# Product-key experts: one-hot tiles with the token innermost and 16-bit operands, weight streams in 1 MB halves

## The chip, the core and the metric

The kernel runs on one core of one Trainium2 chip. Its time is the device time of one launch in microseconds (us); the lower the better. Engines are named as in the profile: PE (TensorE matmuls), PEld (TensorE weight loads), DVE (VectorE), ACT (ScalarE), POOL (GpSimd), SP (the queue that issues the DMAs).

## The reference, cut to what matters

The program is two layers of a mixing stage and a product-key expert stage, then one further mixer and a mixture of 32 experts. The change touches the product-key stage (`_peer`). For 256 tokens, 8 heads and 16 picks a head, it is

```
s    = einsum('thcd,ckd->thck', q, subkeys)        # 2 x 128 key scores a head
sv, si = top_k(s, 16);  cand = sv[..0..] + sv[..1..];  cv, ci = top_k(cand, 16)
experts = ea * 128 + eb                            # ea, eb in 0..127: 16384 experts
gate = softmax(cv)
act  = gelu(einsum('cd,ced->ce', x, u_tab[experts]))
y    = einsum('ce,ced->cd', act * gate, v_tab[experts])
```

Each token uses 128 of the 16,384 experts, and every expert has a row of 1024 numbers in `u_tab` and one in `v_tab`, all float32.

## The kernel before, in words

The product-key stage gathers nothing. It goes through all 16,384 experts in 128 chunks (chunk c holds the experts with second key c, 128 of them, one for each first key), for all 256 tokens, and multiplies by a gate that is zero where a token did not pick an expert. Three kinds of work run on PE:

- **stage 1** (`pe_stage1`, L979): chunk c of `u` times the tokens, float32, 8 products of 128x128 by 128x256, which the profile lists as 16 matmuls. ACT puts the gelu into the slot `c % 76` of the store `H` (`HELD` is 76).
- **build** (`pe_build`, L989): the gates of 16 tokens for 32 chunks. For token i the product of a one-hot over the 128 first keys (`Aoh`) with a one-hot over 32 second keys times the gate (`Boh`, the gate cut into three bf16 parts, k = 0 to 2) gives a 128x32 tile; 16 tokens times 3 parts are 48 matmuls, 128x128 by 128x32 in bf16. There are 64 builds a layer, n = 0 to 63: builds 16q to 16q + 15 are for chunks 32q to 32q + 31. The 128 lanes of `Aoh` and `Boh` are the picks of a token. DVE makes `Aoh` in `dve_keys_hot` (one comparison of 2048 elements a lane) and `Boh` in `dve_gates_hot` (one comparison and three products of 512 elements), and multiplies the built gates into `H` in `dve_gate`. `Aoh`, `Boh` and the result banks are held twice.
- **stage 2** (`pe_stage2`, L998): chunk c of `H` times chunk c of `v`, each cut in a high and a low part by ACT and DVE (`act_split_v`, `dve_split_v`, `dve_split_p`), 12 matmuls of 512 columns. `dve_split_v` of chunk c + 2 waits for stage 2 of chunk c, since `v_lo` is held twice.

The order is written out by hand. PE runs stage 1 for chunks 0 to 31, then 16 times a build and one or two chunks of stage 1 (chunks 32 to 49), and then a loop over c = 0 to 127 of stage 2, into which the other builds and chunks 50 to 127 of stage 1 are put: two chunks of stage 1 for each c up to 24, then one for each c up to 52, and none after that. Builds 16 to 31 stand at c = 8 to 23, builds 32 to 47 at c = 25 to 40, and builds 48 to 63 at every 2.4 chunks from c = 55 to c = 91. DVE makes the first keys' one-hots one or two chunks ahead of the build and the gates' one-hots one chunk ahead. Engines work through their own instruction lists in order, and wait for each other by semaphores.

The weights come through a ring of three places of 2 MB (`Slots`, `load`): a DMA brings four chunks of `u` (when stage 1 comes to a multiple of four) or of `v`, strictly in the order of the list on SP, and each waits until the place's earlier tenant has been given back, which is at the last of its four chunks (`ring.back`). In the loop the order on SP is two pieces of `u` and one of `v` for four chunks. A piece of `v` is given back by `dve_split_v`. While SP waits for one place it issues nothing behind it.

In the arena, `eg` (numbers of the picked keys and gates, float32) and `gs` (the three gate parts, float32) lie in front of `H`; slots of `H` from 50 on (`ROUTED`) lie over the routing scratch, so that gelus from chunk 50 on wait until the routing is over.

Of the kernel before, what the change touches and what calls it, by code (L numbers as in the profile page):

```python
# [17 lines left out]
NSLOT = 3  # L18
PIECE = 4096
HELD = 76  # L20
TURNED = 19
BEFORE = 50
ROUTED = 50
FREE = 1 << 20
# [206 lines left out]


def bc(ap, axis, n):
    ap = ap.unsqueeze(axis)
    shape = list(ap.shape)
    shape[axis] = n
    return ap.broadcast_to(shape)


def build(nc, d, out):  # L240
    with ExitStack() as ctx:
# [50 lines left out]

        ring = Slots([ring_t[:, i * PIECE:(i + 1) * PIECE] for i in range(NSLOT)], at)
        s_ring = [sem(f"ring{i}_landed") for i in range(NSLOT)]
        fills = [0] * NSLOT
        banks = Slots(bank, at)
# [3 lines left out]
        def load(src, cols, *key):  # L300
            buf, (s, n) = ring.take(*key)
            i = ring.place[key]
            fills[i] += 1
            S.wait_ge(s, n)
            S.dma(buf[:, 0:cols], src, s_ring[i])
            at.put(("landed", key), s_ring[i], 16 * fills[i])
# [136 lines left out]
        def pe_mod(j):  # L443
            if j % 6:
                pe_mod_turn(j - 1)
            b, (s, n) = banks.take("mod", j)
            P.wait_ge(s, n)
            P.wait_ge(*at["landed", ("w_mod", j)])
            P.wait_ge(*at["silu c"])
            w = ring.of("w_mod", j).rearrange("p (c n) -> p c n", c=8)  # L450
# [106 lines left out]
        def pe_project_out(l, k, yT, *made):  # L557
            P.wait_ge(*at[made])
            P.wait_ge(*at["landed", ("w_out", l, k)])
            w = ring.of("w_out", l, k).rearrange("p (c n) -> p c n", c=4)  # L560
            for tk in range(2):
                for dh in range(2):
                    b, (s, n) = banks.take("out", l, k, tk, dh)
                    P.wait_ge(s, n)
                    P.mm(b[:, :], [(yT[:, c, tk * 128:tk * 128 + 128], w[:, c, dh * 512:dh * 512 + 512]) for c in range(4)])
                    P.mark("out", l, k, tk, dh)
            ring.back(P, "w_out", l, k)

        def pe_mixing(l):
# [5 lines left out]
            for j in range(4):  # L575
                P.wait_ge(*at["landed", ("w_inA", l, j)])
                w = ring.of("w_inA", l, j).rearrange("p (c n) -> p c n", c=8)
                for half in range(2):
# [338 lines left out]
        top[0] = ARENA - 11200  # L917
        assert H0 + 256 * ROUTED <= top[0]
        pq = [ar3(4, 256) for _ in range(2)]
        ps_ = [ar4(2, 4, 128) for _ in range(4)]  # L920
# [58 lines left out]
        def pe_stage1(l, c):  # L979
            P.wait_ge(*at["landed", ("u", l, c // 4)])  # L980
            if c >= 2:
                P.wait_ge(*at["gelu", l, c - 2])
            w = ring.of("u", l, c // 4).rearrange("p (i c a) -> p i c a", i=4, c=8)
            P.mm(bU[c % 2][:, 0:256], [(w[:, c % 4, dc, :], xT[:, dc, :]) for dc in range(8)])
            P.mark("up", l, c)
            if c % 4 == 3:
                ring.back(P, "u", l, c // 4)
# [22 lines left out]
        def pe_peer(l):  # L1010
            after_stage(P, "mix", l)
            route_banks.restart()
            for j in range(4):
                P.wait_ge(*at["landed", ("wq", l, j)])
                w = ring.of("wq", l, j).rearrange("p (c n) -> p c n", c=8)
                for hf in range(2):
# [120 lines left out]
        def dve_split_v(l, c):  # L1137
            w = ring.of("vt", l, c // 4).rearrange("p (i n) -> p i n", i=4)[:, c % 4, :]
            V.wait_ge(*at["v high", l, c])
# [3 lines left out]
            V.mark("v split", l, c)  # L1143
            if c % 4 == 3:
                ring.back(V, "vt", l, c // 4)

        def dve_peer(l):
# [15 lines left out]
            V.cp(gsb[:, 0, :], eg[:, 2, :])  # L1163
            V.cp(gs[:, 0, :], gsb[:, 0, :])
# [3 lines left out]
            V.tt(gs[:, 2, :], eg[:, 2, :], gs[:, 1, :], SUB)  # L1168
            V.mark("gates split", l)
            for n in range(16):  # L1170
                dve_keys_hot(l, n)
# [48 lines left out]
        def act_split_v(l, c):  # L1220
            A.wait_ge(*at["landed", ("vt", l, c // 4)])
            if c >= 3:
                A.wait_ge(*at["down", l, c - 3])
            A.act(v_hi[c % 3], ring.of("vt", l, c // 4).rearrange("p (i n) -> p i n", i=4)[:, c % 4, :], ACT.Copy)
            A.mark("v high", l, c)
# [41 lines left out]
        def pool_peer(l):  # L1267
            after_stage(G, "mix", l)
            end_stage(G, "G", "peer", l)

# [89 lines left out]
        def pe_task(kind, k, ct):  # L1360
            P.wait_ge(*at["landed", ("w_hg", kind, k)])
            w = ring.of("w_hg", kind, k).rearrange("p (c n) -> p c n", c=8)
            cs = slice(ct * 128, ct * 128 + 128)
# [114 lines left out]
        def pe_mixer():  # L1478
# [16 lines left out]
            P.wait_ge(*at["ckv"])  # L1495
            w = ring.of("w_kvb").rearrange("p (v c n) -> p v c n", v=2, c=2)
            for h in range(8):
# [506 lines left out]
        more_slots = [ar(PIECE) for _ in range((ARENA - top[0]) // PIECE)]  # L2004
        s_ring += [sem(f"ring{NSLOT + i}_landed") for i in range(len(more_slots))]
        top[0] = e_mark
# [28 lines left out]
        def sp_moe():  # L2035
# [4 lines left out]
            once(bgu[0:32, :], d["b_gu"], "b_gu")  # L2040
            for i in range(len(more_slots)):
                ring.bufs.append(more_slots[i])
                ring.tenant.append(None)
                fills.append(0)
            ring.n = NSLOT
            load(d["w_gu"][0, 3], 4096, "w_gu", 0, 1, 1)
# [51 lines left out]
        def pe_up(j, i, k, *gathered):  # L2098
            x = xe[i]
            for v in range(2):  # L2100
# [7 lines left out]
                for h in range(2):  # L2108
                    P.wait_ge(*at["landed", ("w_gu", j, v, h)])
                    w = ring.of("w_gu", j, v, h).rearrange("p (c g n) -> p c g n", c=4, g=2)  # L2110
                    for c in range(4):
# [20 lines left out]
        def pe_down(j):  # L2132
# [3 lines left out]
            for hf in range(2):  # L2136
                P.wait_ge(*at["landed", ("w_dn", j, hf)])
                w = ring.of("w_dn", j, hf).rearrange("p (f n) -> p f n", f=4)
                for f in range(4):
# [375 lines left out]
        def start_ring():  # L2515
            ring.bufs, fills[:] = ring.bufs[0:NSLOT], [0] * NSLOT
            ring.restart()
# [183 lines left out]
```

## Time and profile before

| | before |
|---|---|
| median of 3 runs | 4366.12 us (4361.21 to 4377.41) |
| the profiled execution: time, span | 4377.61 us, 4375.8 us |
| mean granted TensorE clock | 0.944 |
| PE busy | 3942.4 us (90%) |
| DVE busy | 2018.1 us (46%) |
| ACT busy | 895.2 us (20%) |
| POOL busy | 154.4 us (4%) |

The span is one execution, from its first to its last instruction. Busy times are those of instructions that compute; a share is an average over stages with different limits. The product-key stage of the first layer lies at about 250 to 1300 us of the span, that of the second at about 1500 to 2530 us, and the last 1100 us are the 32 experts. The granted clock is 1.00 at the full 2.4 GHz and 0.50 at 1.2 GHz.

### The profile page before, as it was taken

The numbers are of one execution on the slowest core, as the hardware profiler recorded it, in microseconds if no ns is written. First come the engines' busy times: TensorE is split into PE (matmuls) and PEld (weight loads), VectorE is DVE, ScalarE is ACT, GpSimd is POOL, SyncE is SP. The second block draws the span as 40 slices with busy tenths as digits, with TensorE's granted clock in tenths as the row PEclk, the third lists the DMA queues.
The fourth block names the chain that finished last, engine by engine and source line by source line (L and its number), as shares of the span: only waits on it lengthen the run. The fifth ranks groups of instructions, "written<-read, shape, count | busy, mean of one in ns | idle before, by whom it ended". The sixth has DMA issues, their size and how long they took to land.

```text
span 4375.8 us, 54878 instructions
## 1 busy us (share of the span) xinstructions
PE 3942.4 (90%) x23468; PEld 2746.5 (63%) x23468; DVE 2018.1 (46%) x3441; ACT 895.2 (20%) x1502; POOL 154.4 (4%) x135
## 2 busy tenths in 40 slices
PE   6989999998988899999998979998869999999986
PEld 5778878886777688887876756565643333332333
DVE  4276645748754497255758533355532111111112
ACT  2311111223434111212233421223300000000000
POOL 0000000000000000000000000021200000000000
PEclk9799999999998899999999989999979999999998
DMA  4433323443344333333443331211129999999993
GB/s 182 155 135 138 132 116 131 159 155 135 135 165 155 134 137 125 124 136 135 154 154 123 137 127 49 106 58 58 58 81 413 427 428 427 428 427 428 425 398 145
DMA packets 62282, 846.18 MB, mean 193 GB/s; under 512 B 6800, under 2 KB 8976, under 8 KB 10160
## 3 DMA queue, kind: packets, MB, share of 16 engines
q1 hardware_dynamic: 62032, 842.60, 47.9%
q8 instruction: 187, 3.06, 0.3%
q14 instruction: 63, 0.52, 0.0%
HBM read 841.52 MB, written 1.05 MB: 193 GB/s over the span
## 4 chain that ended last, share of the span: by engine, by line
PE 67%; DVE 15%; DMA 13%; ACT 3%; issue 2%; SPq 0%; POOL 0%; DVEq 0%; ACTq 0%
PE bank L83 65%; DVE arena L119 6%; DMA ring<-in_w_gu_dram 6%; DMA ring<-in_peer_u_dram 3%; DMA arena<-in_w_gu_dram 3%; ACT arena L109 2%; DVE vlo L119 2%; PE bank L96 2%; DVE arena L187 1%; DVE arena L181 1%; DVE arena L193 1%; DVE arena L145 1%; DVE arena L133 1%; DVE arena L125 1%; DVE arena L127 1%
## 5 line engine op out<-in xcount | busy, mean ns | idle before, releaser
L83 PE MATMUL bank<-xT,ring 128*128 128x256 f32 x5120 | 1174.1, 389 | 55.7 <-DMA ring<-in_peer_u_dram 33.4
L83 PEld LDWEIGHTS bank<-xT,ring 128*128 128x128 f32 x5120 | 988.2, 195 | 197.8 <-DMA ring<-in_peer_u_dram 35.9
L83 PE MATMUL bank<-arena 128*128 128x32 bf16 (+7 forms) x9660 | 926.6, 291 | 145.7 <-DVE arena L119 108.5
L83 PEld LDWEIGHTS bank<-arena 128*128 128x128 bf16 (+4 forms) x9660 | 544.4, 126 | 522.9 <-issue 294.5
L83 PE MATMUL bank<-ring,arena 128*64 128x512 f32 (+1 forms) x2304 | 592.5, 606 | 39.5 <-DMA ring<-in_w_gu_dram 33.7
L109 ACT ACTIVATE arena<-bank 128x256 f32<-128x256 f32 (+2 forms) x484 | 223.8, 462 | 1975.2 <-PE bank L83 1484.6
L83 PEld LDWEIGHTS bank<-ring,arena 128*64 128x64 f32 (+1 forms) x2304 | 194.4, 146 | 427.3 <-issue 328.5
L119 DVE TENSOR_TENSOR arena<-arena 128x512 bf16<-128x512 bf16 (+6 forms) x636 | 424.4, 703 | 82.0 <-ACT arena L109 67.9
L119 DVE TENSOR_TENSOR vlo<-ring,vhi 128x1024 fp32r<-128x1024 f32 x256 | 313.2, 1224 | 267.2 <-PE bank L83 249.8
L83 PE MATMUL bank<-vhi,phi 128*128 128x512 f32 x1024 | 432.3, 422 | 0.0
L83 PE MATMUL bank<-vhi,plo 128*128 128x512 f32 x1024 | 406.7, 397 | 0.0
L83 PE MATMUL bank<-vlo,phi 128*128 128x512 f32 x1024 | 406.6, 397 | 0.0
L83 PE MATMUL bank<-arena,ring 128*128 128x256 f32 (+2 forms) x1472 | 363.3, 409 | 26.6 <-issue 14.2
L119 DVE TENSOR_TENSOR arena<-cst,arena 128x2048 bf16<-128x2048 f32 (+1 forms) x257 | 372.4, 1481 | 0.0
L83 PEld LDWEIGHTS bank<-arena,ring 128*128 128x128 f32 (+1 forms) x1472 | 253.1, 188 | 129.0 <-issue 91.4
L109 ACT ACTIVATE arena<-arena 128x512 f32<-128x512 f32 (+7 forms) x202 | 134.4, 666 | 797.8 <-DVE arena L125 619.0
L109 ACT ACTIVATE vhi<-ring 128x1024 fp32r<-128x1024 f32 x256 | 272.0, 1063 | 31.4 <-DMA ring<-in_peer_v_dram 20.3
L119 DVE TENSOR_TENSOR plo<-arena,phi 128x256 fp32r<-128x256 f32 x256 | 107.9, 421 | 318.2 <-ACT phi L109 318.2
L139 DVE COPY arena<-bank 128x256 f32<-128x256 f32 (+4 forms) x124 | 70.3, 567 | 387.9 <-PE bank L83 337.1
L83 PEld LDWEIGHTS bank<-vhi,plo 128*128 128x128 f32 x1024 | 197.1, 192 | 44.0
L83 PEld LDWEIGHTS bank<-vlo,phi 128*128 128x128 f32 x1024 | 198.0, 193 | 40.3
L83 PEld LDWEIGHTS bank<-vhi,phi 128*128 128x128 f32 x1024 | 197.5, 193 | 39.6
(105 smaller groups left out, 1665.9 us busy)
## 6 DMA issues: line engine op xcount, KB each, us to landing
ring<-in_w_gu_dram SPq DMA_DIRECT2D x85, 2048.0 KB, 19.3
ring<-in_peer_u_dram SPq DMA_DIRECT2D x64, 2048.0 KB, 8.7
ring<-in_peer_v_dram SPq DMA_DIRECT2D x64, 2048.0 KB, 8.6
arena<-in_w_gu_dram SPq DMA_DIRECT2D x55, 2048.0 KB, 19.4
ring<-in_w_dn_dram SPq DMA_DIRECT2D x41, 2048.0 KB, 17.9
arena<-in_w_dn_dram SPq DMA_DIRECT2D x29, 2048.0 KB, 20.6
ring<-in_w_hg_dram SPq DMA_DIRECT2D x14, 2048.0 KB, 8.6
ring<-in_w_mod_dram SPq DMA_DIRECT2D x12, 2048.0 KB, 7.8
```

The costliest lines, as they stand in the source:

```text
L83: i = self.e.matmul(o, l, r, start=start, stop=stop)
L96: self.e.transpose(o, src, ident[0:n, 0:n]).then_inc(self.sem, 1)
L109: self.e.activation(o, i, f, scale=scale, **kw).then_inc(self.sem, 1)
L119: self.e.tensor_tensor(o, a, b, op).then_inc(self.sem, 1)
L125: self.e.tensor_scalar(o, a, s1, None, o1).then_inc(self.sem, 1)
L127: self.e.tensor_scalar(o, a, s1, s2, o1, o2).then_inc(self.sem, 1)
L133: self.e.scalar_tensor_tensor(out=o, in0=a, scalar=s, in1=b, op0=o1, op1=o2).then_inc(self.sem, 1)
L139: self.e.tensor_copy(o, i).then_inc(self.sem, 1)
L145: self.e.tensor_reduce(o, i, AX.X, op, negate=neg).then_inc(self.sem, 1)
L181: self.e.max(o, i).then_inc(self.sem, 1)
L187: self.e.max_index(o, v, i).then_inc(self.sem, 1)
L193: self.e.match_replace(o, v, i, by).then_inc(self.sem, 1)
```

## The change

- `Aoh`, `Boh` and the comparison tile `eqb` are laid out with the token innermost: an element (key, token) lies at 16 * key + token, where it was at 128 * token + key (32 * token + key for `Boh` and `eqb`). What DVE reads for them becomes bf16 too: `e16` in place of `eg`, `gsb` in place of `gs`, and `keys16`, a bf16 list in which each key's number stands 16 times, in place of `iota`. POOL writes `keys16` once a layer, at the head of the stage; one more DVE copy makes `e16`.
- PE reads one token's one-hots as columns that lie 16 elements (32 bytes) apart, for the stationary operand (128 columns) and for the moving one (32 columns). The number and the order of all matmuls stay.
- The ring has six half places of 1 MB. `u` and `v` come in DMAs of two chunks, 64 and 64 a layer where it was 32 and 32, and each waits for the tenant of its own half. A load of more than 1 MB takes two neighbouring halves, and waits for both.
- `eg` and `gs` move behind `H`, into the scratch; `ROUTED` goes from 50 to 45.

```diff
 PIECE = 4096
+HALF = PIECE // 2
-ROUTED = 50
+ROUTED = 45
...
+class Ring:
+    def __init__(self, places, at):
+        self.places, self.at, self.place = list(places), at, {}
+        self.restart()
+    def restart(self):
+        self.n, self.tenant = 0, [None] * (2 * len(self.places))
+    def take(self, cols, *key):
+        wide = cols > HALF
+        if wide and self.n % 2:
+            self.n += 1
+        i = self.n % len(self.tenant)
+        self.n += 1 + wide
+        before = [k for k in self.tenant[i:i + 1 + wide] if k]
+        self.tenant[i:i + 1 + wide] = [key] * (1 + wide)
+        self.place[key] = i
+        return i, [self.at["back", k] for k in before]
...
         def load(src, cols, *key):
-            buf, (s, n) = ring.take(*key)
-            i = ring.place[key]
+            i, before = ring.take(cols, *key)
             fills[i] += 1
-            S.wait_ge(s, n)
-            S.dma(buf[:, 0:cols], src, s_ring[i])
+            for s, n in before:
+                S.wait_ge(s, n)
+            S.dma(ring.half(i)[:, 0:cols], src, s_ring[i])
...
-        eg = ar4(3, 2, 128).rearrange("p k t n -> p k (t n)")
-        gs = ar4(3, 1, 256).rearrange("p k o n -> p k (o n)")
         gsb = ar(384).bitcast(BF16).rearrange("p (k n) -> p k n", k=3)
+        e16 = ar(256).bitcast(BF16).rearrange("p (c n) -> p c n", c=2)
+        keys16 = ar(1024).bitcast(BF16).rearrange("p (a t) -> p a t", t=16)
...
-        Aoh = [ar(1024).bitcast(BF16).rearrange("p (t a) -> p t a", t=16) for _ in range(2)]
-        Boh = [ar(768).bitcast(BF16).rearrange("p (k t b) -> p k t b", k=3, t=16) for _ in range(2)]
-        eqb = [ar(256).bitcast(BF16).rearrange("p (t b) -> p t b", t=16) for _ in range(2)]
-        top[0] = ARENA - 11200
+        Aoh = [ar(1024).bitcast(BF16).rearrange("p (a t) -> p a t", t=16) for _ in range(2)]
+        Boh = [ar(768).bitcast(BF16).rearrange("p (k b t) -> p k b t", k=3, t=16) for _ in range(2)]
+        eqb = [ar(256).bitcast(BF16).rearrange("p (b t) -> p b t", t=16) for _ in range(2)]
+        top[0] = ARENA - 12736
...
         def sp_u(l, c):
-            if c % 4 == 0:
-                load(d["peer_u"][l, c // 4], 4096, "u", l, c // 4)
+            if c % 2 == 0:
+                load(d["peer_u"][l, c // 4][:, c % 4 * 1024:c % 4 * 1024 + 2048], 2048, "u", l, c // 2)
 
         def sp_v(l, c):
-            if c % 4 == 0 and c < 128:
-                load(d["peer_v"][l, c // 4], 4096, "vt", l, c // 4)
+            if c % 2 == 0 and c < 128:
+                load(d["peer_v"][l, c // 4][:, c % 4 * 1024:c % 4 * 1024 + 2048], 2048, "vt", l, c // 2)
...
-                P.mm(bG[n % 2][:, i * 32:i * 32 + 32], [(ah[:, i, :], bh[:, k, i, :]) for k in range(3)])
+                P.mm(bG[n % 2][:, i * 32:i * 32 + 32], [(ah[:, :, i], bh[:, k, :, i]) for k in range(3)])
...
-            V.tt(Aoh[n % 2], bc(iota, 1, 16), bc(eg[:, 0, t0:t0 + 16], 2, 128), EQ, lag=FREE)
+            V.tt(Aoh[n % 2], keys16, bc(e16[:, 0, t0:t0 + 16], 1, 128), EQ, lag=0 if n < 2 else FREE)
...
-            V.tt(eqb[n % 2], bc(iota[:, q * 32:q * 32 + 32], 1, 16), bc(eg[:, 1, t0:t0 + 16], 2, 32), EQ, lag=FREE)
+            V.tt(eqb[n % 2], keys16[:, 32 * q:32 * q + 32, :], bc(e16[:, 1, t0:t0 + 16], 1, 32), EQ, lag=FREE)
...
-                V.tt(Boh[n % 2][:, k, :, :], eqb[n % 2], bc(gs[:, k, t0:t0 + 16], 2, 32), MUL, lag=k)
+                V.tt(Boh[n % 2][:, k, :, :], eqb[n % 2], bc(gsb[:, k, t0:t0 + 16], 1, 32), MUL, lag=k)
...
         def pool_peer(l):
             after_stage(G, "mix", l)
+            G.cp(keys16, bc(iota, 2, 16))
+            G.mark("keys listed", l)
```

`pe_stage1`, `act_split_v` and `dve_split_v` take their chunk from a half place and give it back at every odd chunk, `dve_peer` waits for "keys listed" ahead of its first comparison, and all other users of the ring read the first 2 MB from their place as before.

## Rows read from the trace of the kernel before

**Rows 1.** The page: busy time of each engine over the whole span.

```profile
PE 3942.4 (90%) x23468; PEld 2746.5 (63%) x23468; DVE 2018.1 (46%) x3441; ACT 895.2 (20%) x1502; POOL 154.4 (4%) x135
```

**Rows 2.** Stretches of the first product-key stage: length, busy us, clock, DMA share, GB/s.

```profile
core 0: us, PE busy (x) PEld busy (x) DVE busy (x) ACT busy (x) POOL busy (x), PEclk, DMA share, GB/s
515.00:830.00 315.00, 296.25 (x2147) 252.22 (x2146) 157.00 (x186) 61.49 (x108) 0.00 (x0) 0.96 0.34 135
830.00:1000.00 170.00, 169.87 (x1264) 144.57 (x1260) 103.68 (x132) 47.87 (x77) 0.00 (x0) 1.00 0.42 158
1000.00:1162.00 162.00, 134.14 (x1208) 108.91 (x1209) 139.29 (x170) 54.70 (x74) 0.00 (x0) 0.92 0.35 130
```

**Rows 3.** Waits of PE, 515:830, 1765:2080, 1000:1162: total us, times, longest us.

```profile
PE bank L83 <- DMA ring<-in_peer_u_dram: 16.0, 6, 5.1
PE bank L83 <- DVE arena L119: 2.8, 1, 2.8
...
PE bank L83 <- DMA ring<-in_peer_u_dram: 17.4, 6, 5.1
...
PE bank L83 <- DVE arena L119: 28.0, 16, 2.2
```

**Rows 4.** Timeline of PE, first builds: start us, us, work, idle before.

```profile
467.02 1.35 PE L83 MATMUL bank<-arena 128*128 128x32 bf16 x48
468.23 3.70 PE L83 MATMUL bank<-xT,ring 128*128 128x256 f32 x16
471.76 1.35 PE L83 MATMUL bank<-arena 128*128 128x32 bf16 x48
...
490.25 1.40 PE L83 MATMUL bank<-arena 128*128 128x32 bf16 x48 [4.07 <-DVE arena L119]
491.48 5.16 PE L83 MATMUL bank<-xT,ring 128*128 128x256 f32 x16
```

**Rows 5.** Groups of DVE instructions over the span, by shape: busy us, mean ns.

```profile
L119 DVE TENSOR_TENSOR vlo<-ring,vhi 128x1024 fp32r<-128x1024 f32 x256 | 313.2, 1224 | 267.2 <-PE bank L83 249.8 <-ACT vhi L109 17.4
L119 DVE TENSOR_TENSOR arena<-cst,arena 128x2048 bf16<-128x2048 f32 x128 | 292.5, 2285 | 0.0
...
L119 DVE TENSOR_TENSOR arena<-arena 128x512 bf16<-128x512 bf16 x384 | 242.6, 687 | 4.4
...
L119 DVE TENSOR_TENSOR plo<-arena,phi 128x256 fp32r<-128x256 f32 x256 | 107.9, 421 | 318.2 <-ACT phi L109 318.2
```

**Rows 6.** Timeline at one wait of PE for `u`, c = 5 to 7.

```profile
564.78 7.07 PE L83 MATMUL bank<-xT,ring 128*128 128x256 f32 x32
...
566.68 5.53 SPq L206 DMA_DIRECT2D ring<-in_peer_u_dram  x2
...
579.76 8.85 PE L83 MATMUL bank<-xT,ring 128*128 128x256 f32 x32 [5.15 <-DMA ring<-in_peer_u_dram]
```

**Rows 7.** Timeline at one of builds 48 to 63.

```profile
1007.89 1.23 DVE L119 TENSOR_TENSOR vlo<-ring,vhi 128x1024 fp32r<-128x1024 f32 x1 [1.13 <-PE bank L83]
...
1009.75 1.90 DVE L119 TENSOR_TENSOR arena<-arena 128x512 bf16<-128x512 bf16 x3
...
1011.79 1.35 PE L83 MATMUL bank<-arena 128*128 128x32 bf16 x48 [1.27 <-DVE arena L119]
```

**Rows 8.** The chain of work in order of time: builds 48 and 63, each layer.

```profile
1002.11 5.68 PE bank L83 x60
...
1158.14 103.74 PE bank L83 x492
...
2252.41 5.24 PE bank L83 x60
...
2405.94 103.21 PE bank L83 x492
```

**Rows 9.** DMA issues of 1 MB: count, KB each, median us to landing.

```profile
ring<-in_cmp_w_dram SPq DMA_DIRECT2D x4, 1024.0 KB, 4.8
```

**Rows 10.** Float32 matmuls: timeline of PE at 136; a group over the span.

```profile
136.39 3.92 PE L83 MATMUL bank<-arena,ring 128*64 128x30 f32 x64
...
L83 PE MATMUL bank<-arena 128*128 128x128 f32 x672 | 101.6, 308 | 33.0 <-DVE arena L119 28.5 <-ACT arena L109 3.7 <-DVE arena L199 0.8
```

More of the change, by code:

```diff
@@ L230, in back, with half, of @@
         self.at.put(("back", key), q.sem, q.n)
+class Ring:
[14 more added lines that the diff above has]
+        return i, [self.at["back", k] for k in before]
+    def half(self, i):
+        return self.places[i // 2][:, i % 2 * HALF:]
+    def of(self, *key):
+        return self.half(self.place.get(key, 0))
+    def back(self, q, *key):
+        self.at.put(("back", key), q.sem, q.n)
 def bc(ap, axis, n):
@@ L291, in par @@
             return pp[:, c:c + n]
-        ring = Slots([ring_t[:, i * PIECE:(i + 1) * PIECE] for i in range(NSLOT)], at)
-        s_ring = [sem(f"ring{i}_landed") for i in range(NSLOT)]
-        fills = [0] * NSLOT
+        ring = Ring([ring_t[:, i * PIECE:(i + 1) * PIECE] for i in range(NSLOT)], at)
+        s_ring = [sem(f"ring{i}_landed") for i in range(2 * NSLOT)]
+        fills = [0] * (2 * NSLOT)
         banks = Slots(bank, at)
@@ L449, in pe_mod @@
             P.wait_ge(*at["silu c"])
-            w = ring.of("w_mod", j).rearrange("p (c n) -> p c n", c=8)
+            w = ring.of("w_mod", j)[:, 0:PIECE].rearrange("p (c n) -> p c n", c=8)
             for dc in range(8):
@@ L559, in pe_project_out @@
             P.wait_ge(*at["landed", ("w_out", l, k)])
-            w = ring.of("w_out", l, k).rearrange("p (c n) -> p c n", c=4)
+            w = ring.of("w_out", l, k)[:, 0:PIECE].rearrange("p (c n) -> p c n", c=4)
             for tk in range(2):
@@ L576, in pe_mixing @@
                 P.wait_ge(*at["landed", ("w_inA", l, j)])
-                w = ring.of("w_inA", l, j).rearrange("p (c n) -> p c n", c=8)
+                w = ring.of("w_inA", l, j)[:, 0:PIECE].rearrange("p (c n) -> p c n", c=8)
                 for half in range(2):
@@ L979, in pe_stage1 @@
         def pe_stage1(l, c):
-            P.wait_ge(*at["landed", ("u", l, c // 4)])
+            P.wait_ge(*at["landed", ("u", l, c // 2)])
             if c >= 2:
                 P.wait_ge(*at["gelu", l, c - 2])
-            w = ring.of("u", l, c // 4).rearrange("p (i c a) -> p i c a", i=4, c=8)
-            P.mm(bU[c % 2][:, 0:256], [(w[:, c % 4, dc, :], xT[:, dc, :]) for dc in range(8)])
+            w = ring.of("u", l, c // 2)[:, 0:HALF].rearrange("p (i c a) -> p i c a", i=2, c=8)
+            P.mm(bU[c % 2][:, 0:256], [(w[:, c % 2, dc, :], xT[:, dc, :]) for dc in range(8)])
             P.mark("up", l, c)
-            if c % 4 == 3:
-                ring.back(P, "u", l, c // 4)
+            if c % 2:
+                ring.back(P, "u", l, c // 2)
         def pe_build(l, n):
@@ L1014, in pe_peer @@
                 P.wait_ge(*at["landed", ("wq", l, j)])
-                w = ring.of("wq", l, j).rearrange("p (c n) -> p c n", c=8)
+                w = ring.of("wq", l, j)[:, 0:PIECE].rearrange("p (c n) -> p c n", c=8)
                 for hf in range(2):
@@ L1137, in dve_split_v @@
         def dve_split_v(l, c):
-            w = ring.of("vt", l, c // 4).rearrange("p (i n) -> p i n", i=4)[:, c % 4, :]
+            w = ring.of("vt", l, c // 2)[:, c % 2 * 1024:c % 2 * 1024 + 1024]
             V.wait_ge(*at["v high", l, c])
@@ L1143, in dve_split_v @@
             V.mark("v split", l, c)
-            if c % 4 == 3:
-                ring.back(V, "vt", l, c // 4)
+            if c % 2:
+                ring.back(V, "vt", l, c // 2)
         def dve_peer(l):
@@ L1163, in dve_peer @@
             V.cp(gsb[:, 0, :], eg[:, 2, :])
-            V.cp(gs[:, 0, :], gsb[:, 0, :])
+            V.cp(e16, eg[:, 0:2, :], lag=1)
+            V.cp(gs[:, 0, :], gsb[:, 0, :], lag=1)
             V.tt(eg[:, 2, :], eg[:, 2, :], gs[:, 0, :], SUB)
@@ L1167, in dve_peer @@
             V.cp(gs[:, 1, :], gsb[:, 1, :])
-            V.tt(gs[:, 2, :], eg[:, 2, :], gs[:, 1, :], SUB)
+            V.tt(gsb[:, 2, :], eg[:, 2, :], gs[:, 1, :], SUB)
             V.mark("gates split", l)
+            V.wait_ge(*at["keys listed", l])
             for n in range(16):
@@ L1220, in act_split_v @@
         def act_split_v(l, c):
-            A.wait_ge(*at["landed", ("vt", l, c // 4)])
+            A.wait_ge(*at["landed", ("vt", l, c // 2)])
             if c >= 3:
                 A.wait_ge(*at["down", l, c - 3])
-            A.act(v_hi[c % 3], ring.of("vt", l, c // 4).rearrange("p (i n) -> p i n", i=4)[:, c % 4, :], ACT.Copy)
+            A.act(v_hi[c % 3], ring.of("vt", l, c // 2)[:, c % 2 * 1024:c % 2 * 1024 + 1024], ACT.Copy)
             A.mark("v high", l, c)
@@ L1361, in pe_task @@
             P.wait_ge(*at["landed", ("w_hg", kind, k)])
-            w = ring.of("w_hg", kind, k).rearrange("p (c n) -> p c n", c=8)
+            w = ring.of("w_hg", kind, k)[:, 0:PIECE].rearrange("p (c n) -> p c n", c=8)
             cs = slice(ct * 128, ct * 128 + 128)
@@ L1495, in pe_mixer @@
             P.wait_ge(*at["ckv"])
-            w = ring.of("w_kvb").rearrange("p (v c n) -> p v c n", v=2, c=2)
+            w = ring.of("w_kvb")[:, 0:PIECE].rearrange("p (v c n) -> p v c n", v=2, c=2)
             for h in range(8):
@@ L2004, in build @@
         more_slots = [ar(PIECE) for _ in range((ARENA - top[0]) // PIECE)]
-        s_ring += [sem(f"ring{NSLOT + i}_landed") for i in range(len(more_slots))]
+        s_ring += [sem(f"ring{2 * NSLOT + i}_landed") for i in range(2 * len(more_slots))]
         top[0] = e_mark
@@ L2040, in sp_moe @@
             once(bgu[0:32, :], d["b_gu"], "b_gu")
[L2041 to L2045, printed above, removed]
+            for place in more_slots:
+                ring.places.append(place)
+                ring.tenant += [None, None]
+                fills.extend([0, 0])
+            ring.n = 2 * NSLOT
             load(d["w_gu"][0, 3], 4096, "w_gu", 0, 1, 1)
@@ L2109, in pe_up @@
                     P.wait_ge(*at["landed", ("w_gu", j, v, h)])
-                    w = ring.of("w_gu", j, v, h).rearrange("p (c g n) -> p c g n", c=4, g=2)
+                    w = ring.of("w_gu", j, v, h)[:, 0:PIECE].rearrange("p (c g n) -> p c g n", c=4, g=2)
                     for c in range(4):
@@ L2137, in pe_down @@
                 P.wait_ge(*at["landed", ("w_dn", j, hf)])
-                w = ring.of("w_dn", j, hf).rearrange("p (f n) -> p f n", f=4)
+                w = ring.of("w_dn", j, hf)[:, 0:PIECE].rearrange("p (f n) -> p f n", f=4)
                 for f in range(4):
@@ L2515, in start_ring @@
         def start_ring():
-            ring.bufs, fills[:] = ring.bufs[0:NSLOT], [0] * NSLOT
+            ring.places, fills[:] = ring.places[0:NSLOT], [0] * (2 * NSLOT)
             ring.restart()
```

2 lines of the change are left out of this document (added).

## The prediction

> **What bounds the kernel now.** I read the busy times first: PE is busy for 90% of the span and DVE for 46% [rows 1]. So work saved on DVE is worth time only where PE waits for DVE, and work added to PE is worth all of its time nearly everywhere. The stretches of the first product-key stage say where [rows 2]: from 830 to 1000 PE is busy for 169.87 of 170 us at the full clock; from 515 to 830 it lacks 19 us and the clock falls to 0.96; from 1000 to 1162 it lacks 28 us at a clock of 0.92. The waits name what is late [rows 3]: 16.0 us for `u` in six waits in the first layer and 17.4 us in six in the second; 28.0 us for DVE in the stretch of builds 48 to 63, the same in the second layer; one wait of 2.8 us. And the first sixteen builds end in a wait of 4.07 us for DVE [rows 4]. The experts at the end are not touched by the edits.
>
> A wait costs more than its length. After 5.15 us of waiting the next 32 matmuls take 8.85 us, where the same 32 take 7.07 at the full clock [rows 6]: 1.8 us more; after 4.07 us the next 16 take 5.16 in place of 3.70 [rows 4], 1.5 more. They start at 1.2 GHz and get back to 2.4.
>
> **1. The halves and the waits for `u`.** Why is `u` late? The place of a piece of `v` comes free at its fourth chunk, in the loop's iterations c = 5, 9, ...; SP waits for it with the next `u` behind. At 566.68 it can issue, and PE, which wants that `u` at c = 7, gets it 13 us later, at 579.76 [rows 6]; two pieces of 2 MB are in flight at once. With half places the list per two iterations is `u`, `v`, `u`, and each load takes the half of the load six before it, from four iterations earlier. The `v` half wanted at iteration c was last used by chunks c - 2 and c - 1, so it is free when stage 2 of c - 3 has run; the `u` behind it can go then and is wanted at c + 1. That is over two iterations, 20 us and more, for a transfer of 1 MB, which lands in 4.8 us [rows 9]. So I take all of the waits for `u` off: 33.4 us. The two waits of 2.8 us go as well (their builds came late because DVE's split stood behind a late `v`): 5.6 us. For the clock, 14 waits at 1.8 us would be 25; the shorter ones give back less, so 20. Sum **59 us**. The number of bytes stays, and a stretch of stage 1 alone needs 1 MB for each 7 us. SP's 64 more issues a layer are behind nothing that PE waits for.
>
> **2. DVE's one-hots.** DVE durations go by elements: 421 ns for 256, 687 for 512, 1224 for 1024, 2285 for 2048 [rows 5], and a product with one 16-bit and one 32-bit input (512 elements, 687 ns) runs no faster than float32. No row shows a two-input operation with all operands 16-bit and contiguous. From below the gain is nothing, from above the number of elements halves: 2285 becomes 1224, and four times 687 becomes 421, 2.1 us a build. I take the half, since what held the product of rows 5 at one element a cycle is its float32 input or its stride, and the change removes both. The Trainium skill ("VectorE: DVE Perf Modes", The perf-mode tier table) says that a `tensor_tensor` of bf16 in SBUF runs at 2x and one of float32 at 1x; by it the durations would be the same halves. The step of 0 that repeats the 16 tokens lies outside the innermost 16 and should not matter.
>
> Where does it pay? In the first sixteen builds: DVE needs one operation of 2285 ns and five of about 687 (the gate's too) for each, 5.7 us, and PE 4.74 (from 467.02 to 471.76 [rows 4]); with 2.1 us less, 3.6, DVE is never late: 4.07 + 1.5, twice, **11 us**. In builds 16 to 47 PE is full already: nothing. In builds 48 to 63: from build 48 to build 63 the first layer takes 1158.14 - 1002.11 = 156.0 us, the second 2405.94 - 2252.41 = 153.5 [rows 8]. PE's own work there is 36 chunks of stage 2 and 15 builds. The last piece of rows 8 is one build and 37 chunks in 103.74 us; less 1.2 for the build, 1.7 for the slow clock and 0.2 of tail, a chunk is 2.72. So 36 x 2.72 + 15 x 1.21 = 116 us, and 40 and 37 us are to be had. DVE keeps some of it: its split of `v` starts at 1007.89 when stage 2 is done, takes 1.23, and then the comparison and the three products must end before the build at 1011.79, 3.9 us later [rows 7]. PE is there 2.72 us after 1007.9. With the halves the chain is 1.23 + 0.42 + 3 x 0.4 = 2.9 us: some 0.25 us is left in each of 30 builds, 7 us. Sum 77 - 7 = **70 us**.
>
> **3. PE's strided operands.** The builds' matmuls read columns 32 bytes apart. Now 48 take 468.23 - 467.02 = 1.21 us, 25.2 ns each [rows 4]. Stage 1 runs 16 matmuls of 256 float32 columns in 3.53 us, 220 ns each, and a stage 2 matmul has 512 columns in 2.72 / 12 = 227 ns: 0.43 ns a column, so 32 columns are 14 ns, and what fills the 25.2 ns is the weight load or a fixed cost an instruction. No row shows a strided operand on PE. From below a stride costs nothing, 25.2 ns. From above the nearest rows are float32: 64 weight columns with 30 moving columns cost 3.92 / 64 = 61 ns, and 128 weight columns with 128 moving ones 101.6 / 672 = 151 ns [rows 10]; in these the weight load shows. I take half rate for the moving columns, 28 ns, and 2 more for the gap between matmuls: 30 ns. That is 48 x 4.8 ns = 0.23 us a build, and there are 128 builds: **-30 us**.
> The Trainium skill speaks against this edit. "SBUF — State Buffer" (Door 1: The DMA port swizzle, the note on cachelines) says that SBUF has lines of 16 bytes, that full bandwidth needs at least two hits in a line, and that an access that goes to a new line pays a penalty; it gives no figure for PE. By it every column of the new layout is a new line, and the first rival below is what would follow if the loads pay it too.
>
> **4. The rest.** POOL's `keys16` runs at the head of the stage, while DVE waits for the first key scores, and is read over 100 us later: nothing; without that cover it would be a few us. The copy to `e16` lies ahead of the first comparison, some 40 us before PE wants the first build: nothing. `ROUTED` 45: those gelus come after several builds, which need the routing over anyway: nothing. The wide loads see the same places as before.
>
> **The sum.** 59 + 11 + 70 - 30 = 110 us. The profiled execution took 4377.6 us, so its like would take 4268; it lies 11.5 us above the median of the runs, and from the median, 4366.1, the forecast is **4256 us**.
>
> **The rivals.**
> A. *The strided weight loads bind PE.* If weights and moving columns both come at a reduced rate and share the time, a matmul takes 48 to 61 ns. It decides from 140 us / 128 / 48 = 23 ns more, 48 ns: from there the kernel is slower. At 55 ns a build costs 1.43 us more, 183 us in all, against the 140: 4409 us; at 61 ns 4446. For it: in rows 10 short matmuls are bound by their loads, and the 25.2 ns hold a load now. Against it: 14 ns of columns leave 11 ns of room for the stream, and load and stream overlap elsewhere (float32 matmuls of 256 columns show no load in their 220 ns). Chance 0.20.
> B. *The quick weight load is lost.* 128 bf16 columns load within 25 ns now, 128 float32 columns in up to 151 [rows 10]. If a stride makes the load go like the latter, at 100 to 151 ns a build costs 3.6 to 6.0 us more, and the time is 4690 to 5000 us. Chance 0.08.
> C. *DVE does not get faster.* Then only part 1 and the PE cost are left: 4366 - 59 + 30 = 4337 us. Chance 0.07.
> D. *`u` is still late.* SP keeps one strict list; if some half is still freed too late, part 1 is lost: 4366 - 81 + 30 = 4315 us. Against it is the lead of two iterations. Chance 0.10.
> The forecast's case has 0.55; alone it lies between 4214 (stride free, no leftover, all of the clock back) and 4340.
>
> **The numbers.** Below 0.5% (22 us) a measurement of this kernel can hardly be told from no change. Faster than 4344: the forecast's case and D, and most of C: 0.70. Within: the rest of C, the edges of A and of the forecast: 0.06. Slower than 4388: most of A, and B: 0.24. The range goes from 4214 up through half of A: 4215 to 4410 leaves out B and the upper half of A, 0.18.
>
> **What would show it.** In the profile after: the comparison of 2048 elements at 1.2 us and those of 512 at 0.42 (C if not); no wait of PE for `u` in the loop (D if there are); the 48 matmuls of a build in 1.2 to 1.5 us, up to 1.9 at 40 ns (2.3 or more is A, 4.8 or more B); 36 chunks and 15 builds, 48 to 63, in about 120 us; PE waiting for nothing for more than 1 us from 515 on. The prediction is wrong above all if a strided matmul costs over 40 ns, and also if a faster DVE and new waits make a pattern in builds 48 to 63 in which PE still stands more than 1 us a build.

## The result, and the profile after

The changed kernel takes 4572.79 us (median of 4 runs, 4563.98 to 4578.18), the kernel before beside it 4368.38. The ratio is 1.0465, with a 95% interval from 1.0439 to 1.0491: 4.65% slower, about 204 us. The forecast was 4256 us, and the range ended at 4410.

Both gains that the forecast counted on are there, and the kernel is slower all the same. The page of the kernel after, busy times:

```profile
PE 4234.4 (93%) x23468; PEld 3029.4 (66%) x23468; DVE 1757.1 (38%) x3443; ACT 894.5 (20%) x1502; POOL 157.6 (3%) x137
```

DVE has 261 us less to do than in [rows 1]; PE has 292 us more, with the same 23468 matmuls. The groups of DVE, by shape:

```profile
L120 DVE TENSOR_TENSOR arena<-arena 128x512 bf16<-128x512 bf16 x512 | 193.7, 419 | 4.4
L120 DVE TENSOR_TENSOR arena<-arena 128x2048 bf16<-128x2048 bf16 x128 | 155.9, 1218 | 0.3
```

1218 ns where it was 2285, and 419 where it was 687 [rows 5]: the durations that the kernel before had for half as many elements, as forecast. The waits of PE in the first product-key stage (280 to 1400 us of the span), to be read against [rows 3]:

```profile
PE bank L97 <- DVE xtok L120: 11.4, 2, 9.8
PE bank L84 <- DVE arena L120: 3.5, 16, 0.2
PE bank L84 <- PE bank L97: 0.7, 1, 0.7
```

No wait for `u` is left, and the builds' waits for DVE are 0.2 us each. The loss is inside the builds. The timeline of PE, two of the first sixteen builds and what follows them, and the granted clock ahead of 493 us and behind it:

```profile
470.22 3.37 PE L84 MATMUL bank<-arena 128*128 128x32 bf16 x48
473.42 3.69 PE L84 MATMUL bank<-xT,ring 128*128 128x256 f32 x16
...
493.58 5.15 PE L84 MATMUL bank<-xT,ring 128*128 128x256 f32 x16
```

```profile
490.50:493.00 2.50, 2.50 (x41) 2.50 (x40) 0.00 (x0) 0.39 (x1) 0.00 (x0) 1.00 0.00 0
493.50:496.50 3.00, 3.00 (x12) 2.44 (x10) 0.69 (x1) 0.00 (x0) 0.00 (x0) 0.50 0.00 0
```

From 470.22 to 473.42 a build's 48 matmuls take 3.20 us, 66.7 ns each, where [rows 4] had 1.21 us, 25.2 ns. And after some builds the 16 matmuls of stage 1 take 5.15 us in place of 3.69, though PE waited for nothing: the clock is 1.00 in the build up to 493 us and 0.50 right behind it, so the strided matmuls of this build ran at the full clock and those after them pay. The stretches of the stage (columns as in [rows 2]):

```profile
core 0: us, PE busy (x) PEld busy (x) DVE busy (x) ACT busy (x) POOL busy (x), PEclk, DMA share, GB/s
...
505.00:1071.00 566.00, 565.97 (x3615) 492.57 (x3615) 200.40 (x330) 110.79 (x190) 0.00 (x0) 0.95 0.35 125
...
1077.00:1252.00 175.00, 171.68 (x1165) 144.04 (x1164) 104.25 (x163) 54.08 (x74) 0.00 (x0) 0.85 0.32 110
```

PE is listed as busy for 565.97 of 566 us, and yet the clock is 0.95; in builds 48 to 63 it is 0.85. Before, with 28 us of waiting in that stretch, it was 0.92 [rows 2]. The chain of work there, builds 48 and 63 of the first layer:

```profile
1076.77 7.80 PE bank L84 x60
...
1251.19 105.63 PE bank L84 x492
```

174.4 us where it was 156.0 [rows 8]. PE's own work at the full clock would be 36 x 2.72 + 15 x 3.20 = 146 us; of the other 28, 3.5 are the waits for DVE, and most of the rest is the clock (0.85 over 175 us is 26 us short of the full clock).

So there are two things to explain: what in the strided read makes a matmul cost 66.7 ns, and why the clock falls with PE always at work.

### The profile page after: what moved, and what is told of

It reads as the page before. It is cut to its first block, busy times and chain, and to the rows that moved or that the text cites. A ratio compares the mean times of both kernels' runs of the same rounds, so it can differ in the third digit from the quotient of the medians.

```text
span 4572.4 us, 55145 instructions
## 1 busy us (share of the span) xinstructions
PE 4234.4 (93%) x23468; PEld 3029.4 (66%) x23468; DVE 1757.1 (38%) x3443; ACT 894.5 (20%) x1502; POOL 157.6 (3%) x137
## 4 chain that ended last, share of the span: by engine, by line
PE 75%; DVE 13%; DMA 9%; ACT 2%; issue 1%; POOL 0%; SPq 0%; DVEq 0%; ACTq 0%
PE bank L84 73%; DMA ring<-in_w_gu_dram 6%; DVE arena L120 4%; DMA arena<-in_w_gu_dram 3%; ACT arena L110 2%; PE bank L97 2%; DVE arena L188 1%; DVE vlo L120 1%; DVE arena L182 1%; DVE arena L194 1%; DVE arena L146 1%; DVE arena L134 1%; DVE arena L126 1%; DVE arena L128 1%; DVE arena L152 0%
## 5 line engine op out<-in xcount | busy, mean ns | idle before, releaser
L84 PE MATMUL bank<-arena 128*128 128x32 bf16 (+7 forms) x9660 | 1178.9, 337 | 84.2 <-DVE arena L120 46.2
L84 PE MATMUL bank<-xT,ring 128*128 128x256 f32 x5120 | 1197.5, 394 | 22.3 <-DMA mq<-in_mq_dram 18.7
L84 PEld LDWEIGHTS bank<-xT,ring 128*128 128x128 f32 x5120 | 1009.9, 199 | 168.5 <-issue 20.8
L84 PEld LDWEIGHTS bank<-arena 128*128 128x128 bf16 (+4 forms) x9660 | 791.5, 163 | 458.4 <-issue 300.8
L120 DVE TENSOR_TENSOR arena<-arena 128x512 bf16<-128x512 bf16 (+5 forms) x892 | 522.8, 620 | 84.9 <-ACT arena L110 70.7
L84 PE MATMUL bank<-vhi,phi 128*128 128x512 f32 x1024 | 444.4, 434 | 0.0
L84 PE MATMUL bank<-vlo,phi 128*128 128x512 f32 x1024 | 416.1, 406 | 0.0
L84 PE MATMUL bank<-vhi,plo 128*128 128x512 f32 x1024 | 415.9, 406 | 0.0
L120 DVE TENSOR_TENSOR arena<-arena,bank 128x512 f32<-128x512 f32 (+2 forms) x164 | 92.8, 582 | 396.8 <-PE bank L84 396.8
```

The lines of the kernel that those rows point to most:

```text
L84: i = self.e.matmul(o, l, r, start=start, stop=stop)
L120: self.e.tensor_tensor(o, a, b, op).then_inc(self.sem, 1)
```

## The experiments

Times of kernels with several rounds are medians, with the ratio to the kernel before on the same chip; the others are one run each (the kernel before ran at 4370.2, 4371.8 and 4366.3 beside them). A matmul's time in a build is the distance from the build's start to the start of what follows, over its number of matmuls, at the full clock.

### The halves alone

```diff
 # the kernel before, with Ring, HALF and the loads of the change; one-hots as before
-                load(d["peer_u"][l, c // 4], 4096, "u", l, c // 4)
+                load(d["peer_u"][l, c // 4][:, c % 4 * 1024:c % 4 * 1024 + 2048], 2048, "u", l, c // 2)
```

> The kernel before with the ring of six half places alone; one-hots as before (float32 inputs, key innermost). Theory of the prediction's part 1: no wait of PE for u in the loop (33.4 us before), the two 2.8 us waits gone, some clock back: 4368 - 59 = 4309 us. Rival (u late for another reason, or smaller transfers are less efficient): PE still waits for u and the time is 4368 or above. Builds at 25 ns a matmul in both.

4292.63 us, ratio 0.9831 (0.9811 to 0.9850): 78 us faster, 19 more than the sum had. The waits of PE from 480 to 970 of the span:

```profile
PE bank L84 <- DVE arena L120: 4.1, 1, 4.1
```

No wait for `u`, and the 2.8 us wait is gone too; the 4.1 us are those of [rows 4] at the fourteenth build. The clock is the point that the sum had too low:

```profile
515.00:970.00 455.00, 453.47 (x3404) 388.85 (x3402) 261.92 (x320) 110.58 (x187) 0.00 (x0) 1.00 0.42 151
```

1.00 where [rows 2] show 0.96. The waits were 38.9 us in the two layers; the other 39 us are what came after them, mostly the clock: over the whole span the mean granted clock was 0.954, where the kernel before had 0.944 in the run of median time beside it. I had put 20.

### The one-hots alone

```diff
 # the changed kernel with
-                load(d["peer_u"][l, c // 4][:, c % 4 * 1024:c % 4 * 1024 + 2048], 2048, "u", l, c // 2)
+                load(d["peer_u"][l, c // 4], 4096, "u", l, c // 4)      # and v likewise
```

> The changed kernel with u and v in whole 2 MB pieces again; token innermost and bf16 kept. If the loss is the strided builds alone (67 ns a matmul, 255 us) this takes as long as the changed kernel plus the waits for u that come back, 0 to 59 us: 4573 to 4632. If the halves are part of the loss it is below 4573.

4586.76 us, ratio 1.0498 (1.0478 to 1.0518). The loss is the one-hots'; the halves take 14 us off it, which is not clear of the noise: the intervals of the two ratios overlap (1.0478 to 1.0518 here, 1.0439 to 1.0491 for the change). PE's waits in the loop of the first layer:

```profile
PE bank L84 <- DMA ring<-in_peer_u_dram: 5.6, 2, 5.3
PE bank L84 <- DVE arena L120: 0.5, 2, 0.2
```

With builds of 3.20 us the whole pieces come nearly in time, so the halves have little left to take away.

### All bf16, but contiguous for PE

The run of contiguous 16-bit elements that DVE wants need not be 16 tokens: two are enough. Each token's number and gates are written twice side by side (`e2`, `f2`, `g2`), the one-hots lie as before, and DVE goes through them in pairs of keys.

```diff
-            V.tt(Aoh[n % 2], keys16, bc(e16[:, 0, t0:t0 + 16], 1, 128), EQ, ...)
+            V.tt(Aoh[n % 2][:, :, :, 0].rearrange("p t (h r) -> p t h r", r=2),
+                 bc(iota16.rearrange("p (h r) -> p h r", r=2), 1, 16), bc(e2[:, t0:t0 + 16, :], 2, 64), EQ, ...)
...
+            V.cp(e2, bc(eg[:, 0, :], 2, 2), lag=1)      # f2 from eg[:, 1], g2 from gsb likewise
...
-                P.mm(..., [(ah[:, :, i], bh[:, k, :, i]) for k in range(3)])
+                P.mm(..., [(ah[:, i, :], bh[:, k, i, :]) for k in range(3)])    # key innermost
```

> Halves as in the change, all DVE operands bf16, but the one-hots lie with the key innermost as before, so that PE reads contiguous columns; DVE gets its contiguous innermost step from each token's number and gates written twice side by side, and compares and multiplies in pairs of keys. Theory (PE's stride is the whole loss, and parts 1 and 2 of the sum hold): builds at 25 ns a matmul, DVE's 2048-element comparison at 1.22 us, and 4368 - 140 = 4228 us. Rival 1 (a run of two elements does not get DVE's double rate): comparison at 2.29 us, 4309 us. Rival 2 (the clock or PE's matmuls suffer from DVE's faster writes): builds still slower than 40 ns, above 4400 us.

4227.18 us, ratio 0.9682 (0.9660 to 0.9704): faster than both kernels, and within 1 us of the expectation. Its timeline of PE, its group of comparisons, and the chain from the fourteenth build on, with the last piece of builds 48 to 63:

```profile
457.89 1.35 PE L84 MATMUL bank<-arena 128*128 128x32 bf16 x48
459.09 3.70 PE L84 MATMUL bank<-xT,ring 128*128 128x256 f32 x16
```

```profile
L120 DVE TENSOR_TENSOR arena<-arena 128x2048 bf16<-128x2048 bf16 x128 | 156.0, 1219 | 0.1
```

```profile
483.72 471.22 PE bank L84 x3612
...
1084.22 102.13 PE bank L84 x492
```

A build's matmul takes 25.0 ns, the comparison 1219 ns, and the 3612 matmuls that took 565.67 us after the change take 471.22. Everything in the sum but the strided read is in this kernel, and the sum without that term, 4366 - 140 = 4226, comes out. That it does so to 1 us is luck, since two of its terms are off by 19 and 16 us in opposite directions (below). A build keeps its 25 ns a matmul beside DVE's faster operations.

### Which operand, and how far apart

All kernels of this part are the one with pairs, with one operand of the builds' matmuls laid out with W tokens innermost (W elements from column to column):

```diff
 # stationary operand, W = 16, 8, 4, 2:   Aoh as "p (g a t) -> p g a t", t=W
+                P.mm(..., [(ah[:, i // W, :, i % W], bh[:, k, i, :]) for k in range(3)])
 # moving operand, W = 16, 4:             Boh as "p (k g b t) -> p k g b t", t=W
+                P.mm(..., [(ah[:, i, :], bh[:, k, i // W, :, i % W]) for k in range(3)])
```

> As the changed kernel, but only the stationary operand (128 columns of the keys' one-hots) keeps its stride of 32 bytes; the moving operand (32 columns) is contiguous. If the stride costs in the weight load: builds near 67 ns a matmul, about 4573 us. If it costs in the moving columns: 25 ns, about 4228 us. If each has a share, between.

> As the changed kernel, but only the moving operand (32 columns) keeps its stride of 32 bytes; the stationary one is contiguous. With the stationary stride alone a matmul of a build took 61.3 ns, with both 66.7, contiguous 25.2. If the moving stride is hidden under the 25 ns: about 4227 us, as with both contiguous. If it adds its 5.4 ns by itself: 30.6 ns and 4260 us. If it is as dear as the stationary one: above 4400 us.

> Stationary operand alone, with 8 elements (16 bytes) from column to column in place of 16. Theory L (lines of 16 bytes decide): each column is still a new line, 61 ns a matmul, 4569 us. Theory P (any gap between columns ends the quick weight load): the same 61 ns. Only a cost that grows with the distance would give less.

> Stationary operand alone, with 2 elements (4 bytes) from column to column; four columns share 16 bytes. Theory L: full rate, 25 ns a matmul, 4227 us. Theory P: 61 ns, 4569 us.

> Stationary operand alone, with 4 elements (8 bytes) from column to column, two columns in 16 bytes; the moving one contiguous. A stride of 2 elements took 25.0 ns a matmul, of 8 elements 59.8, of 16 elements 61.3. Theory T (every 16 bytes touched cost about 1.9 ns in each of four streams of 32 columns, so 16 of them cost 30 ns): 30 ns a matmul. Theory L (two hits in a line are full rate): 25 ns. If the cost goes with the distance: about 40 ns.

> Moving operand alone, with 4 elements (8 bytes) from column to column; with 16 elements it took 59.6 ns a matmul. Theory T: 16 lines of 16 bytes, 30 ns. Theory L: 25 ns. By distance: about 40 ns.

The timelines of PE, a build and the start of what follows it, in this order: stationary W = 16, moving W = 16, stationary W = 8, W = 2, W = 4, moving W = 4.

```profile
454.87 3.09 PE L84 MATMUL bank<-arena 128*128 128x32 bf16 x48
457.81 3.70 PE L84 MATMUL bank<-xT,ring 128*128 128x256 f32 x16
```

```profile
449.13 3.04 PE L84 MATMUL bank<-arena 128*128 128x32 bf16 x48
451.99 3.69 PE L84 MATMUL bank<-xT,ring 128*128 128x256 f32 x16
```

```profile
452.86 3.02 PE L84 MATMUL bank<-arena 128*128 128x32 bf16 x48
455.73 3.70 PE L84 MATMUL bank<-xT,ring 128*128 128x256 f32 x16
```

```profile
463.10 1.35 PE L84 MATMUL bank<-arena 128*128 128x32 bf16 x48
464.30 3.70 PE L84 MATMUL bank<-xT,ring 128*128 128x256 f32 x16
```

```profile
457.59 1.75 PE L84 MATMUL bank<-arena 128*128 128x32 bf16 x48
459.18 3.70 PE L84 MATMUL bank<-xT,ring 128*128 128x256 f32 x16
```

```profile
442.33 1.69 PE L84 MATMUL bank<-arena 128*128 128x32 bf16 x48
443.86 3.70 PE L84 MATMUL bank<-xT,ring 128*128 128x256 f32 x16
```

The distances over 48 give the third column. "More than pairs" is the time less 4227.2; the builds' share is 6144 matmuls times what one takes over 25.0 ns.

| stationary, bytes apart | moving, bytes apart | ns a matmul | time, us | more than pairs | of it the builds | the rest |
|---|---|---|---|---|---|---|
| 2 (contiguous) | 2 | 25.0 | 4227.2 | | | |
| 4 | 2 | 25.0 | 4248.5 | 21 | 0 | 21 |
| 8 | 2 | 33.1 | 4277.4 | 50 | 50 | 0 |
| 2 | 8 | 31.9 | 4276.1 | 49 | 42 | 7 |
| 16 | 2 | 59.8 | 4522.6 | 295 | 214 | 82 |
| 32 | 2 | 61.3 | 4568.7 | 342 | 223 | 118 |
| 2 | 32 | 59.6 | 4508.8 | 282 | 213 | 69 |
| 32 | 32 (the change) | 66.7 | 4572.8 | 346 | 256 | 89 |

Three things follow. First, my expectation for the moving operand alone was a miss: I thought that with both strides at 66.7 and the stationary one at 61.3 the moving one could have little share, 5.4 ns at most, or be hidden. Alone it costs 59.6. Each operand by itself holds the matmul at about 60 ns, and both together at 66.7: they overlap almost wholly. To undo one of them is worth little of the 346 us: 4 us when the moving operand is made contiguous, 64 when the stationary one is (one run each). Second, the distance matters up to 16 bytes and hardly beyond: 25, 33, 60, 61 ns for a stationary stride of 4, 8, 16 and 32 bytes. The cost goes with the number of 16-byte lines that 32 columns touch: 32 lines take 59.6 to 61.3 ns, 1.9 ns each; 16 lines take 31.9 and 33.1, 2.0 each; 8 lines would be 16 ns, hidden under the 25. Theory T (each 16-byte line touched costs 1.9 ns) comes within 3 ns of all rows with one strided operand. Theory L (two columns in a line are full rate) misses the 8-byte rows by 7 to 8 ns, theory P (any gap loses the quick load) misses the row with 4 bytes by 36, and a cost that simply grows with the distance, expected at 40 ns for 8 bytes, misses there by 7 to 8 and has no reason to stop at 16 bytes. That lines are the cause is the reading that fits best; the rows show the times. Third, 128 stationary columns take as long as 32 moving ones, as if they came in four streams of 32 side by side; no run here tests that by itself.

The Trainium skill's "SBUF — State Buffer" (Door 1: The DMA port swizzle, cachelines) has 16-byte lines with a penalty for each change of line, and full bandwidth with two hits in a line: the first half agrees with this table, the second doesn't quite, since with two columns in a line a matmul costs 32 to 33 ns and not 25. The Trainium skill's "TensorE: Matmul & The Clock Gate" (Weight-path perf modes) has the fast weight load read four chunks of 32 columns, packed or strided; 61.3 ns for 128 columns beside 59.6 for 32 agrees with four chunks at once.

The stationary operand at 16 bytes came out at 59.8 ns, near the 61 expected, but at 4522.6 us, 46 below the time expected: 9 us of that are the builds and 37 the rest.

The row with 4 bytes has 21 us that are not PE's reads: there DVE's comparison took longer, since I had it read the key list in runs of two elements that lie 32 bytes apart. Its group of comparisons:

```profile
L120 DVE TENSOR_TENSOR arena<-arena 128x2048 bf16<-128x2048 bf16 x128 | 259.9, 2030 | 0.3
```

2030 ns where the runs of 4, 8 and 16 elements and the pairs had 1219. PE waited 24.4 us for DVE at its builds in place of 11.5, and lost some clock with it.

### The clock

> The changed kernel, each build with two of the three gate parts: the third part's 16 matmuls are left out, so the gates lose their last bits. A build takes 32 x 66.7 ns = 2.13 us in place of 3.20. If the builds cost only their own length: 128 x 1.07 = 137 us less, 4436 us. If long builds also lower the clock for what follows, and builds of 2.13 us do so less often: more than 137 us less, down to 4380 us, with 16 matmuls of stage 1 after a build at 3.5 us in place of 5.0.

```diff
 # the changed kernel, the third gate part left out of every build
-                P.mm(..., [(ah[:, :, i], bh[:, k, :, i]) for k in range(3)])
+                P.mm(..., [(ah[:, :, i], bh[:, k, :, i]) for k in range(2)])
```

4366.5 us: 206 less than the changed kernel. The timeline of PE and the stretch that answers to 505:1071 of the changed kernel:

```profile
448.39 2.27 PE L84 MATMUL bank<-arena 128*128 128x32 bf16 x32
450.48 3.69 PE L84 MATMUL bank<-xT,ring 128*128 128x256 f32 x16
```

```profile
498.00:1002.00 504.00, 503.96 (x3050) 437.11 (x3051) 199.86 (x329) 110.26 (x189) 0.00 (x0) 1.00 0.40 140
```

A build is 2.09 us, the matmuls in it are about as slow as before (65 ns), and the clock is 1.00 in this stretch. A build is 1.11 us shorter, 142 us in all; the other 64 of the 206 us are what builds of 3.20 us cost beyond their own length, more than builds of 2.09 do. The time is 14 us below the lowest that I expected. But the clock is not spared everywhere. Builds 48 to 63 of this kernel:

```profile
1008.00:1158.00 150.00, 146.67 (x914) 120.91 (x912) 103.73 (x163) 53.50 (x72) 0.00 (x0) 0.91 0.38 127
```

0.91, where the kernel with pairs has 1.00 in the same builds and the changed kernel 0.85.

> The kernel with pairs of keys (all contiguous, 4227 us), each build's 48 matmuls run three times over with the same result, so that a build is 3.60 us long, longer than the strided one of 3.20 us, but PE is fed at full rate. If the clock falls after the strided builds because PE stands waiting for operands inside them, it stays up here: 4227 + 128 x 2.40 = 4534 us, and 16 matmuls of stage 1 after a build take 3.5 us. If any long run of narrow matmuls lowers it, some 90 us more, about 4625 us, and 5 us for the 16 after many builds.

```diff
 # the kernel with pairs, each build run three times over
+            for again in range(3):
                 for i in range(16):
                     P.mm(...)
```

4546.8 us, 13 above the expectation for a clock that stays up and 78 below the one for a clock that falls. PE's timeline and the clock:

```profile
448.25 3.70 PE L84 MATMUL bank<-xT,ring 128*128 128x256 f32 x16
451.78 3.75 PE L84 MATMUL bank<-arena 128*128 128x32 bf16 x144
455.38 3.70 PE L84 MATMUL bank<-xT,ring 128*128 128x256 f32 x16
```

```profile
505.00:1071.00 566.00, 566.00 (x7150) 498.79 (x7149) 208.31 (x340) 115.25 (x197) 0.00 (x0) 1.00 0.37 130
```

Builds of 3.60 us of contiguous matmuls leave the clock at 1.00 here (0.98 in builds 48 to 63, which have waits of their own), and the 320 us more than with pairs are 307 of matmuls and 12 others. So neither the length of a build nor its narrow matmuls lower the clock by themselves: builds of 3.60 us at 25 ns a matmul leave it alone, builds of 3.20 us at 67 ns do not. Nor does a stride by itself: builds of 2.09 us at 65 ns lower it only in builds 48 to 63, and the two kernels with 8 bytes between columns, with builds of 1.5 to 1.6 us, have 1.00 in both stretches. The clock fell where long builds of matmuls were held up by their operands, and PE's busy time doesn't tell the two apart. What exactly the clock goes by is not shown.

The whole spans say the same. Span times (1 - mean granted clock) is the time that the clock was short of the full one: 293 us in the changed kernel, 177 with pairs, 210 with two gate parts, 177 with the builds thrice. Between the changed kernel and the one with pairs that is about 115 us, an upper bound for what the clock can have cost, and the table's 89 us lie below it.

### The halves with fast builds

```diff
 # the kernel with pairs, u and v in whole pieces
```

> The kernel with pairs of keys, with u and v in whole 2 MB pieces again. With slow builds the halves were worth 14 us (4587 against 4573), beside the one-hots of before 78 us (4370 against 4293). With fast builds the ring is under its old pressure: the waits of PE for u are back, 33 us and the clock after them, and the time is about 4227 + 70 = 4297 us. If instead DVE's lateness was what made the halves pay, 4240 us.

4283.69 us, ratio 0.9815 (0.9799 to 0.9832): the halves are worth 56.5 us here, 78 with the one-hots of before, about 14 with the strided ones. The expectation was 4297 us. The waits of PE from 480 to 1100 of the span:

```profile
PE bank L84 <- DMA ring<-in_peer_u_dram: 16.5, 6, 5.6
PE bank L84 <- DVE arena L120: 6.3, 17, 2.0
```

The six waits for `u` are back.

## Why the prediction was wrong

**The step that failed** is part 3: "I take half rate for the moving columns, 28 ns, and 2 more for the gap between matmuls: 30 ns." The mechanism was named and the term was in the sum, but mis-sized: -30 us where the strided reads cost 256 us at 66.7 ns a matmul. The choice of half rate had no row behind it; a line of 16 bytes takes 1.9 ns, so one column in each is less than a quarter of the contiguous rate of 0.43 ns a column, and neither the stationary nor the moving read is hidden. Rival A had the mechanism nearly as it is (loads and columns both bind, though they overlap and do not share the time) and even its dearest end, 61 ns and 4446 us, was too low.

**What no part had** is the clock. I let the clock fall only after waits. The strided builds lowered it with PE listed as busy. The 89 us of the 346 between the changed kernel and the one with pairs that are not the builds' own length are put down to it; 64 of these go when the builds have two parts only. Without it rival A at 66.7 ns would have been 4366 - 140 + 256 = 4482.

**Part 1 was right**: no wait for `u` or `v` in the loop. Its size was 78 us by itself and not 59, the clock being the difference; in the changed kernel it is about 14, within the noise, since slow builds had already eased the ring.

**Part 2 was right in its durations and too large in its worth**: 1218 and 419 ns; 0.2 us left at each of builds 48 to 63 as worked out (3.5 us in 16). With pairs against the halves alone it is worth 65 us, where 11 + 70 had been put down. "DVE is never late" holds for the changed kernel only because its builds are slow: with pairs 1.97 us of the 4.07 are left at the fourteenth build, and the first sixteen give about 7 us and not 11. Builds 48 to 63 take 151.9 us with the halves alone and 123.6 with pairs: 57 us in the two layers and not 70, a part of which the halves had already taken from 156.0. The halves alone had been worth 19 more than forecast, so the two errors nearly cancel.

**Part 4 was right**: PE's waits show nothing for `keys16` or `e16`, and the kernel with pairs reaches its time with `ROUTED` at 39. No run changes `ROUTED` by itself.

**The sum** for what is not strided, 140 us, is measured as 143 by the kernel with pairs (4370.2 to 4227.2). Rivals B, C and D did not happen: no strided matmul took 100 ns, DVE became faster, and no `u` was late.

**The chances.** 0.24 for slower was too little. The one unknown price multiplied 6144 matmuls on an engine that was busy 90% of the time, its rows reached from 25 to 151 ns, and the kernel turned slower at 48. With bounds like these the value near the cheap end should not have carried more than half of the chance.

## What to carry to other kernels

A layout has two readers: before the fast side of DVE is bought with a stride for PE, count the 16-byte lines that PE touches for each 32 columns, at about 1.9 ns a line in these runs, against the 25 ns that a short matmul took anyway. DVE had its double rate here with innermost runs of two contiguous 16-bit elements, and a value written twice side by side gives them without moving the key out of the innermost place; but a list read in runs of two that lie 32 bytes apart took 2030 ns and not 1219. A price that stands on the busiest engine and is multiplied by thousands deserves a probe or a wide range.

## What the runs showed of the hardware that was not expected

- A matmul whose operand columns lie 16 bytes or more apart takes about 60 ns with either operand strided and 66.7 with both; at 8 bytes 32 to 33; at 4 bytes 25.0, as contiguous.
- The granted clock can fall while PE is listed as busy without a gap: from 1.00 to 0.50 behind a strided build at 493 us, and 0.95 and 0.85 over the stretches of the changed kernel, where more and longer, but contiguous, builds had 1.00 and 0.98. Strided builds of 2.09 us had 1.00 and 0.91.
- Which stride costs how much clock is not settled: 69 us with the moving operand alone at 32 bytes, 82 and 118 with the stationary one at 16 and 32, 89 with both. These are single runs apart from the last, and builds of almost equal length; the split into builds and rest is an estimate from the time of one build.
- A two-input DVE operation of 2048 bf16 elements took 1219 ns when its inputs came in contiguous runs of 4, 8 or 16, or in pairs of neighbouring keys, but 2030 ns with an input in runs of two elements 32 bytes apart.
